# The first transfers, transposes and splits of an input projection by single k-tiles, and the next x transposes inside its first two half-groups

## The chip, the core and the metric

The kernel runs on one core of one Trainium2 chip. Four compute engines work beside each other: TensorE (PE in the rows; its weight loads are PEld), VectorE (DVE), ScalarE (ACT) and GpSimd (POOL). SyncE (SP) issues nearly all DMAs, which 16 DMA engines carry out. The metric is the device time of one execution in microseconds (us), less is better. Times are medians of three runs.

## What is computed

One decoder layer over 256 tokens of width 2048, in float32. The part that matters here is the beginning, the normed input projection:

```python
def rmsnorm(x, g):
    xf = x.astype(jnp.float32)
    r = lax.rsqrt(jnp.mean(xf * xf, axis=-1, keepdims=True) + EPS)
    return (xf * r).astype(x.dtype) * g
...
    h = rmsnorm(x, norm_mix_g[l])
    proj = jnp.einsum('bsd,de->bse', h, w_in[l])
    dq, dk, dv, mq, mk, mv, gate = jnp.split(proj, SPLITS, axis=-1)
```

`w_in` is 2048 x 8192. Behind it follow eight differential-attention heads, eight heads of ordinary causal attention (with 256 tokens there is one block), the gate, an output projection with `w_out`, a cross-attention to `mem` with four heads, and a last RMSNorm. All of that is the same before and after.

## The kernel before, in words

**Three products for one.** A float32 product is made from rounded parts. Of each weight tile, ScalarE makes `w_hi` (a rounded copy of `w_raw`) and VectorE makes `w_lo = w_raw - w_hi`. The input x is transposed by TensorE into PSUM; ScalarE scales it by the gain and writes `aT_hi`, and VectorE writes `aT_lo`, the rest. TensorE then adds hi times hi, hi times lo and lo times hi.

**Half-groups.** The contraction over 2048 rows goes by 16 k-tiles of 128. Two k-tiles with 512 columns of weights (512 KB) are a half-group. One pair of heads takes 16 half-groups, numbered n = 0 to 15 in `pair_window`; n = 0 to 7 make q and k, transposed, in `project_qk`: for each of the two k-tiles four matmuls of 512 columns with `w_hi` (L501) and four of 256 columns with `w_lo` (L509). n = 8 to 15 make v and the gate (`half_group`).

**Buffers.** `w_raw` has eight slots of a half-group, `w_hi` and `w_lo` four. SP issues the loads in order in `load_pair_half`, two DMAs of 256 KB for each half-group, one for each block of 256 columns. x comes in five parts, `X_PARTS`, between the loads of weights: 256, 256, 512, 512 and 512 columns.

**Blocks.** x is transposed in four blocks of four k-tiles (`transpose_block`, L483). A block has two banks of PSUM, two k-tiles in each, so eight transposes. `block_made` counts banks that TensorE has transposed, `block_hi` those that ScalarE has done (`block_hi_bank`, L753, two operations of 256 columns), `block_lo` those that VectorE has done (`block_lo_bank`, L971, two operations). A half-group n of the first pair waits in `pair_window` for `block_lo` n + 1: it reads just the two k-tiles of one bank.

**The order at the start.** Every engine runs its own list in order. On TensorE it is: `keep_busy(5)`, which are matmuls on an identity tile that compute nothing (L462), the transpose of the gain, the first bank of x, `keep_busy(4)`, the second bank, `keep_busy(2)`, half-group 0, block 1, half-groups 1 and 2, block 2, half-groups 3 and 4, block 3, and so on. On ScalarE and VectorE a bank of x and the split of a half-group of weights take turns. Only half-group 0 is split by k-tile (L740, L741, L954, L957); its two DMAs count on one semaphore, so both k-tiles wait for both. Behind half-group 7 TensorE transposes the row scales (L589), which VectorE makes from the sums of squares of x. A matmul record of `keep_busy` is half of one call: five calls are ten records.

Of the kernel before, what the change touches and what calls it, by code (L numbers as in the profile page):

```python
# [22 lines left out]
F32 = mybir.dt.float32  # L23
# [69 lines left out]
X_PARTS = ((0, 256), (256, 512), (512, 1024), (1024, 1536), (1536, 2048))  # L93
WARM_UP = (5, 4, 2)
# [14 lines left out]
def program(nc, x, mem, norm_mix_g, w_in, lambda_q1, lambda_k1, lambda_q2, lambda_k2,  # L109
            subln_g, w_out, norm_mem_g, mem_norm_g, w_q_mem, w_kv_mem, w_o_mem, final_g, out):  # L110
    with ExitStack() as ctx:
# [135 lines left out]
        first_hi = sem("first_hi")  # L247
        first_lo = sem("first_lo")
# [95 lines left out]
        def _(sp):  # L344
# [92 lines left out]
        def _(pe):  # L437
            def half_group(half, slot, banks, hi, lo, k0, first, last):


                first_half = isinstance(half, int) and half == 0
                if first_half:
                    pe.wait_ge(first_lo, 1)
                else:
                    wait(pe, lo_made, half + 1)
                for k in range(GK // 2):
                    if first_half and k == 1:
                        pe.wait_ge(lo_made, 1)
# [15 lines left out]
            def transpose_block(b):  # L464
# [4 lines left out]
                if source == "x" and n > 0:  # L469
                    pe.wait_ge(x_loaded[n + 1], 16)  # L470
# [6 lines left out]
                for i in range(2):  # L477
                    if source == "x" and n == 0:
                        pe.wait_ge(x_loaded[i], 16)
# [6 lines left out]
                    if source == "x" and n == 0:  # L486
                        keep_busy(WARM_UP[1 + i])

            def project_qk(half, slot, k0, first, last):


                first_half = isinstance(half, int) and half == 0
                if first_half:
                    pe.wait_ge(first_hi, 1)
                else:
                    wait(pe, lo_made, half + 1)
                for k in range(GK // 2):
                    if first_half and k == 1:
                        pe.wait_ge(hi_made, 1)
# [3 lines left out]
                    if first_half:  # L503
                        if k == 0:
                            pe.wait_ge(first_lo, 1)
                        else:
                            pe.wait_ge(lo_made, 1)
# [53 lines left out]
            def pair_window(j, kind, first=False):  # L561

                for n in range(PAIR_HALVES):
# [7 lines left out]
                    if n < PAIR_HALVES // 2:  # L571
                        if first:
# [6 lines left out]
                    if first:  # L579
                        if n in (0, 2, 4):  # L580
# [18 lines left out]
            transpose_block(0)  # L599
# [127 lines left out]
        def _(act):  # L727
            def split_hi(half, i, turn, tail=False):

                act.wait_ge(half_loaded[i % RAW], 32 * (turn + i // RAW + 1))  # L730
                raw = w_raw[:, i % RAW]
# [6 lines left out]
                if isinstance(half, int) and half == 0:  # L738
# [573 lines left out]
```

## Time and profile before

| | us |
|---|---|
| median of 3 runs | 599.54 (599.49 to 599.58) |
| the profiled execution | 600.03 |
| its span, first to last instruction | 598.2 |
| TensorE busy | 586.5 (98%) |
| TensorE weight loads | 499.3 (83%) |
| VectorE busy | 423.3 (71%) |
| ScalarE busy | 321.2 (54%) |
| first matmul of the projection starts | 8.38 |
| first matmul of half-group 1 starts | 12.19 |
| first matmul of half-group 2 starts | 15.12 |

The profiled execution took 1.83 us more than its span and 0.49 us more than the median. A share of busy time is a mean over all stages; for a change at the start the timeline of the first microseconds and the places where TensorE sits idle say more.

### The profile page before, as it was taken

How to read it: one execution, taken by the hardware profiler on the slowest of the kernel's cores; microseconds unless marked ns; L12 is line 12 of the kernel's file. 1: busy time of each engine (PE TensorE's matmuls, PEld its weight loads, DVE VectorE, ACT ScalarE, POOL GpSimd, SP SyncE). 2: the span in 40 equal slices, each digit the busy share in tenths (PEclk: the TensorE clock that was granted, in tenths of full speed). 3: DMA queues.
4: the chain of work that ended last, by engine and by line, in shares of the span. 5: the costliest groups of instructions: out<-in, count | busy, mean ns of one | idle time of the engine just before them, and what ended most of it. 6: DMA issues, size and time to landing. Idle time of an engine off the chain costs nothing.

```text
span 598.2 us, 9295 instructions
## 1 busy us (share of the span) xinstructions
PE 586.5 (98%) x3070; PEld 499.3 (83%) x3070; DVE 423.3 (71%) x709; ACT 321.2 (54%) x549; POOL 17.6 (3%) x41
## 2 busy tenths in 40 slices
PE   8999999999999999999999999999999999999994
PEld 7888888888888888888888888888888888888883
DVE  4698789779788787487676765856566656655875
ACT  5765555546536645545455454553457565544723
POOL 2001001001000100100100100000000000000000
PEclk9999999999999999999999999999999999999998
DMA  8976555554554556555554657645555555454303
GB/s 274 327 255 204 183 169 166 193 175 150 196 171 155 181 167 210 175 167 168 192 175 145 206 173 262 223 171 188 177 177 176 169 182 195 165 198 147 106 1 141
DMA packets 91261, 108.51 MB, mean 181 GB/s; under 512 B 6962, under 2 KB 73059, under 8 KB 90723
## 3 DMA queue, kind: packets, MB, share of 16 engines
q1 hardware_dynamic: 91202, 108.18, 54.8%
q8 instruction: 14, 0.23, 0.2%
q14 instruction: 13, 0.10, 0.0%
q10 hardware_dynamic: 32, 0.01, 0.0%
HBM read 106.06 MB, written 2.10 MB: 181 GB/s over the span
## 4 chain that ended last, share of the span: by engine, by line
PE 96%; DVE 1%; ACT 1%; DMA 1%; issue 0%; SPq 0%; ACTq 0%; DVEq 0%
PE ps L501 19%; PE ps L452 18%; PE ps L454 18%; PE ps L453 18%; PE ps L509 10%; PE ps L550 2%; PE ps L483 2%; PE ps L708 1%; PE ps L712 1%; PE ps L707 1%; PE ps L524 1%; PE ps L538 1%; DMA xs<-in_x 1%; PE ps L681 1%; PE ps L557 1%; PE ps L661 1%
## 5 line engine op out<-in xcount | busy, mean ns | idle before, releaser
L961 DVE TENSOR_TENSOR w_lo<-w_raw,w_hi 128x1024 fp32r<-128x1024 f32 x187 | 229.0, 1226 | 108.1 <-ACT w_hi L743 106.9
L743 ACT ACTIVATE w_hi<-w_raw 128x1024 fp32r<-128x1024 f32 x187 | 198.2, 1062 | 169.9 <-PE ps L454 92.0
L501 PE MATMUL ps<-aT,w_hi 128*128 128x512 f32 x512 | 141.1, 397 | 0.0
L452 PE MATMUL ps<-w_hi,aT 128*128 128x512 f32 x320 | 126.6, 395 | 0.0
L453 PE MATMUL ps<-w_lo,aT 128*128 128x512 f32 x320 | 124.8, 390 | 0.0
L454 PE MATMUL ps<-w_hi,aT 128*128 128x512 f32 x320 | 124.7, 390 | 0.0
L501 PEld LDWEIGHTS ps<-aT,w_hi 128*128 128x128 f32 x512 | 87.3, 189 | 11.7
L509 PEld LDWEIGHTS ps<-aT,w_lo 128*128 128x128 f32 x512 | 78.4, 189 | 10.9
L509 PE MATMUL ps<-aT,w_lo 128*128 128x256 f32 x512 | 81.3, 281 | 0.0
L454 PEld LDWEIGHTS ps<-w_hi,aT 128*128 128x128 f32 x320 | 60.1, 188 | 12.7
L452 PEld LDWEIGHTS ps<-w_hi,aT 128*128 128x128 f32 x320 | 60.1, 188 | 12.3
L453 PEld LDWEIGHTS ps<-w_lo,aT 128*128 128x128 f32 x320 | 60.1, 188 | 11.9
L452 PE MATMUL ps<-w_hi,yT_hi 128*128 128x512 f32 x128 | 50.7, 396 | 0.0
L454 PE MATMUL ps<-w_hi,yT_lo 128*128 128x512 f32 x128 | 49.9, 390 | 0.0
L453 PE MATMUL ps<-w_lo,yT_hi 128*128 128x512 f32 x128 | 49.8, 389 | 0.0
L998 DVE RECIPROCAL pool<-pool 128x128 f32<-128x128 f32 x32 | 30.5, 953 | 1.1
L783 ACT ACTIVATE pool<-pool,small 128x256 f32<-128x256 f32 (+1 forms) x48 | 21.3, 445 | 16.1 <-DVE small L1037 16.1
L454 PEld LDWEIGHTS ps<-w_hi,yT_lo 128*128 128x128 f32 x128 | 24.0, 188 | 5.1
L453 PEld LDWEIGHTS ps<-w_lo,yT_hi 128*128 128x128 f32 x128 | 24.1, 188 | 4.7
L452 PEld LDWEIGHTS ps<-w_hi,yT_hi 128*128 128x128 f32 x128 | 24.1, 188 | 4.7
L428 POOL TENSOR_TENSOR alibi<-dist,slopes 128x256 f32<-128x256 f32 x16 | 15.7, 1000 | 320.7 <-DVE small L1037 320.7
L971 DVE SCALAR_TENSOR_TENSOR aT<-ps,gainsT,aT 128x256 fp32r<-128x256 f32 x32 | 14.0, 479 | 13.1 <-ACT aT L753 13.1
(168 smaller groups left out, 551.6 us busy)
## 6 DMA issues: line engine op xcount, KB each, us to landing
w_raw<-in_w_in SPq DMA_DIRECT2D x256, 256.0 KB, 2.8
w_raw<-in_w_out SPq DMA_DIRECT2D x64, 256.0 KB, 3.3
w_raw<-in_w_kv_mem SPq DMA_DIRECT2D x32, 256.0 KB, 2.9
w_raw<-in_w_q_mem SPq DMA_DIRECT2D x16, 256.0 KB, 2.9
w_raw<-in_w_o_mem SPq DMA_DIRECT2D x16, 256.0 KB, 3.3
mems<-in_mem SPq DMA_DIRECT2D x1, 2048.0 KB, 10.2
xs<-in_x SPq DMA_DIRECT2D x3, 512.0 KB, 7.5
w_raw<-in_final_g SPq DMA_DIRECT2D x1, 1024.0 KB, 4.7
```

What stands on the lines that cost most here:

```text
L428: pool_e.tensor_tensor(alibi[:, u], dist[:, :], slope, ALU.mult).then_inc(alibi_ready, 1)
L452: pe.matmul(acc, hi[:, k0 + k, tok], w_hi[:, slot, k], start=first and k == 0, stop=False)
L453: pe.matmul(acc, hi[:, k0 + k, tok], w_lo[:, slot, k], start=False, stop=False)
L454: m = pe.matmul(acc, lo[:, k0 + k, tok], w_hi[:, slot, k], start=False, stop=last and k == GK // 2 - 1)
L483: m = pe.transpose(ps[:, bank + i, (k * NT + t) * P:(k * NT + t + 1) * P], rows_of[:, t, col:col + P], ident[:, :])
L501: pe.matmul(ps[:, c, :], w_hi[:, slot, k, c * P:(c + 1) * P], aT[:, k0 + k].rearrange("p i s -> p (i s)"), start=first and k == 0, stop=False)
L509: m = pe.matmul(ps[:, c, 0:SEQ], w_lo[:, slot, k, c * P:(c + 1) * P], aT_hi[:, k0 + k, :], start=False, stop=last and k == GK // 2 - 1)
L743: act.activation(w_hi[:, i % SPLITS], raw, ACT.Copy).then_inc(hi_made, 1)
L783: m = act.activation(prob_sb[:, u, c, cols], prob_sb[:, u, c, cols], ACT.Exp, bias=neg_max[:, u, t, c:c + 1], accum_out=exp_sum[:, c, u, t ...
L961: dve.tensor_tensor(lo, w_raw[:, i % RAW], hi.bitcast(F32), ALU.subtract).then_inc(lo_made, 1)
L971: m = dve.scalar_tensor_tensor(lo, ps[:, bank + i, (k % 2) * SEQ:(k % 2 + 1) * SEQ], gainsT[:, gain:gain + 1], hi.bitcast(F32), ALU.mult, ...
L998: dve.reciprocal(s, s).then_inc(silu_steps, 1)
```

## The change

It touches the first two half-groups of the first pair and the x transposes that come before half-group 2.

- **Transfers.** The first two parts of x are one k-tile each (128 columns, 128 KB), and there are seven parts instead of five. Half-groups 0 and 1 are loaded by k-tile: the first k-tile of each in one DMA of 256 KB with a semaphore of its own (`k_loaded`), the second in two DMAs of 128 KB.
- **Transposes.** The first bank of block 0 is split in two: `transpose_first(0)` ahead of the projection, `transpose_first(1)` behind the first four matmuls of half-group 0. The second bank of block 0 moves behind the four matmuls with `w_hi` of the second k-tile of half-group 0. The first bank of block 1 moves into half-group 1, the second behind it. Blocks 2 and 3 stay.
- **Splits.** ScalarE and VectorE do k-tile 0 of x, k-tile 0 of the weights, k-tile 1 of x, k-tile 1 of the weights, then bank 1 of block 0 and half-group 1, this too by k-tile.
- **Matmuls on the identity tile.** Three calls ahead of the gain's transpose instead of five, four behind the first transposes, and none behind that.

```diff
-X_PARTS = ((0, 256), (256, 512), (512, 1024), (1024, 1536), (1536, 2048))
-WARM_UP = (5, 4, 2)
+X_PARTS = ((0, 128), (128, 256), (256, 512), (512, 768), (768, 1024), (1024, 1536), (1536, 2048))
+X_PART_OF = {(1, 0): 3, (1, 1): 4, (2, 0): 5, (3, 0): 6}
+WARM_UP = (3, 4)
...
+            def load_pair_rows(n, k):
+
+                if k == 0:
+                    sp.dma_start(w_raw[:, n, 0, :].rearrange("p (s c) -> p s c", c=2 * P),
+                                 in_slabs[n][:, 0, 0:2, 0:2 * P]).then_inc(k_loaded[n], 16)
+                else:
+                    for part, slab in enumerate(SLABS["diff", 0]):
+                        sp.dma_start(w_raw[:, n, 1, part * 2 * P:(part + 1) * 2 * P], in_slabs[n][:, 1, slab, 0:2 * P]
+                                     ).then_inc(half_loaded[n], 16)
+
             load_x(0)
-            for n in range(PAIR_HALVES):
+            for n in range(2):
+                load_pair_rows(n, 0)
+                if n == 0:
+                    load_x(1)
+                load_pair_rows(n, 1)
+                load_x(2 + n)
+            for n in range(2, PAIR_HALVES):
                 load_pair_half(DIFF, 0, 0, n)
-                if n in (0, 1, 3, 5):
-                    load_x((n + 1) // 2 + 1)
+                if n in (2, 3, 5):
+                    load_x({2: 4, 3: 5, 5: 6}[n])
...
+            def transpose_first(k):
+
+
+                pe.wait_ge(x_loaded[k], 16)
+                for t in range(NT):
+                    m = pe.transpose(ps[:, 6 - 2 * k, (k * NT + t) * P:(k * NT + t + 1) * P],
+                                     xs[:, t, k * P:(k + 1) * P], ident[:, :])
+                m.then_inc(k_made if k == 0 else block_made, 1)
...
+                early = half if isinstance(half, int) and half < 2 else None
+                if early is None:
                     wait(pe, lo_made, half + 1)
                 for k in range(GK // 2):
+                    if early is not None and k == 0:
+                        if early == 0:
+                            pe.wait_ge(k_block_lo, 1)
+                        pe.wait_ge(k_hi, early + 1)
+                    if early is not None and k == 1:
+                        pe.wait_ge(block_lo, early + 1)
+                        pe.wait_ge(hi_made, early + 1)
                     for c in range(4):
                         pe.matmul(ps[:, c, :], w_hi[:, slot, k, c * P:(c + 1) * P],
                                   aT[:, k0 + k].rearrange("p i s -> p (i s)"), start=first and k == 0, stop=False)
+                    if early == 0:
                         if k == 0:
+                            transpose_first(1)
                         else:
+                            transpose_block(0, (1,))
+                    if early == 1 and k == 0:
+                        transpose_block(1, (0,))
...
-                        if first:
+                        if first and n > 0:
                             pe.wait_ge(block_lo, n + 1)
...
                     if first:
-                        if n in (0, 2, 4):
+                        if n == 1:
+                            transpose_block(1, (1,))
+                        if n in (2, 4):
                             transpose_block(1 + n // 2)
...
             def split_hi(half, i, turn, tail=False):
 
+                raw = w_raw[:, i % RAW]
+                if isinstance(half, int) and half < 2:
+
+                    act.wait_ge(k_loaded[half], 16)
+                    act.activation(w_hi[:, half, 0], raw[:, 0], ACT.Copy).then_inc(k_hi, 1)
+                    if half == 0:
+                        block_hi_first(1)
+                    act.wait_ge(half_loaded[half], 32)
+                    act.activation(w_hi[:, half, 1], raw[:, 1], ACT.Copy).then_inc(hi_made, 1)
+                    return
```

The first rows of TensorE before, from the transpose of the gain to half-group 1 (L483 are transposes of x, L462 the matmuls on the identity tile, L501 and L509 the projection with `w_hi` and `w_lo`; the branch rows of the small loops are the last three of each loop):

```order
L483 MATMUL ps<-ident,xs 128x128 [waits x_loaded1]
L483 MATMUL ps<-ident,xs 128x128 x3
L461 UNCONDITIONAL_BRANCH
L462 MATMUL ps<-ident 128x128
L461 REGISTER_ALU
L461 COMPARE_AND_BRANCH
L501 MATMUL ps<-aT,w_hi 128x512 [waits first_hi,block_lo]
L501 MATMUL ps<-aT,w_hi 128x512 x3
L509 MATMUL ps<-aT,w_lo 128x256 [waits first_lo]
L509 MATMUL ps<-aT,w_lo 128x256 x3
L501 MATMUL ps<-aT,w_hi 128x512 [waits hi_made]
L501 MATMUL ps<-aT,w_hi 128x512 x3
```

Both banks of block 0 are transposed ahead of the first L501, and nothing stands between the groups of half-group 0.

The same place on TensorE now, from the first matmul of half-group 0 to the first of half-group 1 (L484 and L507 are transposes of x, L526 and L541 what L501 and L509 were):

```order
L526 MATMUL ps<-aT,w_hi 128x512 [waits k_hi,k_block_lo]
L526 MATMUL ps<-aT,w_hi 128x512 x3
L484 MATMUL ps<-ident,xs 128x128 [waits x_loaded1]
L484 MATMUL ps<-ident,xs 128x128
L541 MATMUL ps<-aT,w_lo 128x256 [waits k_lo]
L541 MATMUL ps<-aT,w_lo 128x256 x3
L526 MATMUL ps<-aT,w_hi 128x512 [waits hi_made,block_lo]
L526 MATMUL ps<-aT,w_hi 128x512 x3
L507 MATMUL ps<-ident,xs 128x128 [waits x_loaded2]
L507 MATMUL ps<-ident,xs 128x128 x3
L541 MATMUL ps<-aT,w_lo 128x256 [waits lo_made]
L541 MATMUL ps<-aT,w_lo 128x256 x3
```

The two transposes of k-tile 1 stand between k-tile 0's groups, and the four of bank 1 behind the L526 of k-tile 1.

What comes next on TensorE now, half-group 1 up to the first matmul of half-group 2:

```order
L526 MATMUL ps<-aT,w_hi 128x512 [waits k_hi,block_lo]
L526 MATMUL ps<-aT,w_hi 128x512 x3
L507 MATMUL ps<-ident,xs 128x128 [waits x_loaded3]
L507 MATMUL ps<-ident,xs 128x128 x3
L541 MATMUL ps<-aT,w_lo 128x256 [waits k_lo]
L541 MATMUL ps<-aT,w_lo 128x256 x3
L526 MATMUL ps<-aT,w_hi 128x512 [waits hi_made,block_lo]
L526 MATMUL ps<-aT,w_hi 128x512 x3
L541 MATMUL ps<-aT,w_lo 128x256 [waits lo_made]
L541 MATMUL ps<-aT,w_lo 128x256 x3
L507 MATMUL ps<-ident,xs 128x128 [waits x_loaded4]
L507 MATMUL ps<-ident,xs 128x128 x3
```

Block 1, which stood ahead of half-group 1, now stands half inside it and half behind it; half-group 2 follows.

ScalarE before, from its first operation on x to the weights of half-group 2 (L753 is x, the others are weights):

```order
L753 ACTIVATE aT<-ps,gainsT 128x256 [waits block_made,gainsT_ready]
L753 ACTIVATE aT<-ps,gainsT 128x256
L740 ACTIVATE w_hi<-w_raw 128x512 [waits half_loaded0]
L741 ACTIVATE w_hi<-w_raw 128x512
L753 ACTIVATE aT<-ps,gainsT 128x256 [waits block_made]
L753 ACTIVATE aT<-ps,gainsT 128x256
L743 ACTIVATE w_hi<-w_raw 128x1024 [waits half_loaded1]
L753 ACTIVATE aT<-ps,gainsT 128x256 [waits block_made]
L753 ACTIVATE aT<-ps,gainsT 128x256
L743 ACTIVATE w_hi<-w_raw 128x1024 [waits half_loaded2]
```

And ScalarE now (L790 and L801 are x, L769, L773 and L782 weights):

```order
L790 ACTIVATE aT<-ps,gainsT 128x256 [waits k_made,gainsT_ready]
L769 ACTIVATE w_hi<-w_raw 128x512 [waits k_loaded0]
L790 ACTIVATE aT<-ps,gainsT 128x256 [waits block_made]
L773 ACTIVATE w_hi<-w_raw 128x512 [waits half_loaded0]
L801 ACTIVATE aT<-ps,gainsT 128x256 [waits block_made]
L801 ACTIVATE aT<-ps,gainsT 128x256
L769 ACTIVATE w_hi<-w_raw 128x512 [waits k_loaded1]
L773 ACTIVATE w_hi<-w_raw 128x512 [waits half_loaded1]
L801 ACTIVATE aT<-ps,gainsT 128x256 [waits block_made]
L801 ACTIVATE aT<-ps,gainsT 128x256
L782 ACTIVATE w_hi<-w_raw 128x1024 [waits half_loaded2]
```

The weights of half-group 1 still stand behind bank 1 of block 0, and those of half-group 2 behind the first bank of block 1. VectorE has the same order, each operation behind ScalarE's of the same name.

## Rows read from the trace of the kernel before

**Rows 1.** Waits of TensorE over the whole span: us in total, times, longest.

```profile
PE ps L483 <- DMA xs<-in_x: 0.8, 1, 0.8
PE ps L589 <- DVE pool L1138: 0.5, 1, 0.5
```

**Rows 2.** Stretches, us from the start: length, then busy us of each engine.

```profile
8.37:15.10 6.73, 6.73 (x43) 5.86 (x42) 4.76 (x8) 4.94 (x9) 0.00 (x0) 1.00 1.04 349
...
34.75:598.20 563.45, 554.78 (x2886) 471.32 (x2886) 403.07 (x668) 297.87 (x515) 14.49 (x14) 1.00 0.53 174
```

**Rows 3.** Chain that ended last, first microseconds: start, us, what.

```profile
2.28 5.19 DMA xs<-in_x
...
8.62 0.93 PE ps L501 x4
9.55 0.47 PE ps L509 x4
...
11.42 0.87 PE ps L483 x8
```

**Rows 4.** Timeline to 9 us: start, us, engine, line, operation, count [idle before].

```profile
0.75 0.45 SPq L360 DMA_DIRECT2D xs<-in_x  x1
1.25 0.98 SPq L354 DMA_DIRECT2D w_raw<-in_w_in  x2
...
1.74 2.50 PE L462 MATMUL ps<-ident 128*128 128x128 f32 x10 [1.74 <-POOL ident L411]
...
4.38 1.11 PE L483 MATMUL ps<-ident,xs 128*128 128x128 f32 x4
...
5.60 0.84 ACT L753 ACTIVATE aT<-ps,gainsT 128x256 fp32r<-128x256 f32 x2 [2.87 <-PE ps L483]
6.56 0.88 DVE L971 SCALAR_TENSOR_TENSOR aT<-ps,gainsT,aT 128x256 fp32r<-128x256 f32 x2 [1.90 <-ACT aT L753]
6.85 0.63 ACT L740 ACTIVATE w_hi<-w_raw 128x512 fp32r<-128x512 f32 x1 [0.41 <-DMA w_raw<-in_w_in]
...
7.51 0.66 PE L483 MATMUL ps<-ident,xs 128*128 128x128 f32 x4 [0.79 <-DMA xs<-in_x]
...
8.38 1.17 PE L501 MATMUL ps<-aT,w_hi 128*128 128x512 f32 x4
```

**Rows 5.** One DMA each, from issue to landing: size, us (last number).

```profile
xs<-in_x SPq DMA_DIRECT2D x1, 256.0 KB, 2.8
mix_gain<-in_norm_mix_g ACTq DMA_DIRECT2D x1, 8.0 KB, 2.2
...
w_raw<-in_w_in SPq DMA_DIRECT2D x1, 256.0 KB, 3.5
...
w_raw<-in_w_in SPq DMA_DIRECT2D x1, 256.0 KB, 5.1
```

**Rows 6.** Single records of L462, and the core's mean granted clock.

```profile
5.29 0.42 PE L462 MATMUL ps<-ident 128*128 128x128 f32 x1
...
8.01 0.28 PE L462 MATMUL ps<-ident 128*128 128x128 f32 x1
...
core 0: 598.2 us, clock 0.996
```

**Rows 7.** Timeline, 11 to 15.2 us: from block 1 to half-group 2.

```profile
11.26 1.04 PE L483 MATMUL ps<-ident,xs 128*128 128x128 f32 x8
...
11.90 0.84 ACT L753 ACTIVATE aT<-ps,gainsT 128x256 fp32r<-128x256 f32 x2 [1.12 <-PE ps L483]
...
12.65 1.06 ACT L743 ACTIVATE w_hi<-w_raw 128x1024 fp32r<-128x1024 f32 x1
12.77 0.88 DVE L971 SCALAR_TENSOR_TENSOR aT<-ps,gainsT,aT 128x256 fp32r<-128x256 f32 x2 [0.73 <-ACT aT L753]
...
13.75 1.23 DVE L961 TENSOR_TENSOR w_lo<-w_raw,w_hi 128x1024 fp32r<-128x1024 f32 x1
...
15.12 1.17 PE L501 MATMUL ps<-aT,w_hi 128*128 128x512 f32 x4
```

**Rows 8.** Timeline further on: half-group 4's load, and block 3.

```profile
17.00 1.06 ACT L743 ACTIVATE w_hi<-w_raw 128x1024 fp32r<-128x1024 f32 x1 [1.60 <-DMA w_raw<-in_w_in]
...
21.68 1.09 PE L501 MATMUL ps<-aT,w_hi 128*128 128x512 f32 x4
...
25.18 0.84 ACT L753 ACTIVATE aT<-ps,gainsT 128x256 fp32r<-128x256 f32 x2 [0.92 <-PE ps L483]
```

More of the change, by code:

```diff
@@ L246, in program @@
         half_loaded = [sem(f"half_loaded{s}") for s in range(RAW)]
[L247 to L248 removed]
+        k_loaded = [sem("k_loaded0"), sem("k_loaded1")]
+        k_made = sem("k_made")
+        k_block_hi = sem("k_block_hi")
+        k_block_lo = sem("k_block_lo")
+        k_hi = sem("k_hi")
+        k_lo = sem("k_lo")
         hi_made = sem("hi_made")
@@ L438, in half_group @@
             def half_group(half, slot, banks, hi, lo, k0, first, last):
[L441 to L445, printed above, removed]
+                wait(pe, lo_made, half + 1)
                 for k in range(GK // 2):
-                    if first_half and k == 1:
-                        pe.wait_ge(lo_made, 1)
                     for t in range(NT):
@@ L476, in transpose_block @@
                     pe.wait_ge(block_lo, 2 * (before[-1] + 1))
-                for i in range(2):
+                for i in banks:
+                    if (n, i) in X_PART_OF and source == "x":
+                        pe.wait_ge(x_loaded[X_PART_OF[n, i]], 16)
                     if source == "x" and n == 0:
-                        pe.wait_ge(x_loaded[i], 16)
+                        pe.wait_ge(x_loaded[2], 16)
                     for k in range(2):
@@ L737, in split_hi, with block_hi_first @@
                 wait(act, half_done, half - behind + 1)
-                if isinstance(half, int) and half == 0:
-                    act.activation(w_hi[:, 0, 0], raw[:, 0], ACT.Copy).then_inc(first_hi, 1)
-                    act.activation(w_hi[:, 0, 1], raw[:, 1], ACT.Copy).then_inc(hi_made, 1)
-                    return
                 act.activation(w_hi[:, i % SPLITS], raw, ACT.Copy).then_inc(hi_made, 1)
+            def block_hi_first(k):
+                if k == 0:
+                    act.wait_ge(k_made, 1)
+                else:
+                    act.wait_ge(block_made, 1)
+                act.activation(aT_hi[:, k], ps[:, 6 - 2 * k, k * SEQ:(k + 1) * SEQ], ACT.Identity,
+                               scale=gainsT[:, k:k + 1]).then_inc(k_block_hi if k == 0 else block_hi, 1)
             def block_hi_bank(b, i):
@@ L950, in split_lo @@
                 lo = wo_lo[:, i - WO_HALF0] if over_yT else w_lo[:, i % SPLITS]
-                if isinstance(half, int) and half == 0:
-                    dve.wait_ge(first_hi, 1)
-                    dve.tensor_tensor(lo[:, 0], w_raw[:, 0, 0], hi[:, 0].bitcast(F32), ALU.subtract
-                                      ).then_inc(first_lo, 1)
-                    dve.wait_ge(hi_made, 1)
-                    dve.tensor_tensor(lo[:, 1], w_raw[:, 0, 1], hi[:, 1].bitcast(F32), ALU.subtract
+                if isinstance(half, int) and half < 2:
+                    dve.wait_ge(k_hi, half + 1)
+                    dve.tensor_tensor(lo[:, 0], w_raw[:, half, 0], hi[:, 0].bitcast(F32), ALU.subtract
+                                      ).then_inc(k_lo, 1)
+                    if half == 0:
+                        block_lo_first(1)
+                    dve.wait_ge(hi_made, half + 1)
+                    dve.tensor_tensor(lo[:, 1], w_raw[:, half, 1], hi[:, 1].bitcast(F32), ALU.subtract
                                       ).then_inc(lo_made, 1)
```

36 lines of the change are left out of this document (18 added, 18 removed).

## The prediction, made before the changed kernel had run

> **What bounds the kernel now.** I read the waits of TensorE first. After its start it waits only twice: 0.8 us for the second part of x and 0.5 us for the row scales behind half-group 7 [rows 1]. The stretches agree: from 8.37 to 15.10 it is busy all 6.73 us, and of the 563.45 us behind 34.75 us it is idle for 8.67 [rows 2], all of it at the end of the kernel, when no matmul is left. So TensorE sets the time, and a microsecond that its work of the first stage ends sooner or later is a microsecond of the whole.
>
> What the start waits for is in the chain that ended last: the second part of x, issued at 2.28, lands 5.19 us later, at 7.47 [rows 3]. The timeline shows the rest: four transposes at 7.51, two calls on the identity tile, then the first projection matmul at 8.38. The first k-tile's `w_hi` was ready at 6.85 + 0.63 = 7.48 and bank 0 of x at 6.56 + 0.88 = 7.44 [rows 4]. Three things thus came in at the same moment, and the change has to speed up all of them.
>
> The second thing to see is that the engines behind TensorE are nearly as late as it is. Block 1's transposes start at 11.26, ScalarE takes its first bank at 11.90, the weights of half-group 2 at 12.65, VectorE their rest at 13.75, done at 14.98, and half-group 2 starts at 15.12 [rows 7]. TensorE had in that time 0.87 for eight transposes and 2 x (0.93 + 0.47) = 2.80 for half-group 1 [rows 3], 3.67 of 3.86 us. So **from the start of the first bank of block 1 to half-group 2 it takes 3.86 us, whatever TensorE does meanwhile**, because half-group 2's weights stand behind that bank on both engines. The change keeps this order. Half-group 2 is therefore the place to measure at: behind it nothing is moved.
>
> **The change part by part.**
>
> **The start.** Three calls instead of five: ten records took 2.50 us [rows 4], some 0.24 each, six take 1.5 and end at 3.2. The gain's transfer, issued at 0.74, lands 2.2 later at 2.9 [rows 5]; its transpose costs 0.2. The first part of x, 256 KB, landed 0.75 + 2.8 = 3.55 [rows 4, 5]; half of that lands no later, so the two transposes go at 3.5. Four took from 4.38 to ScalarE's 5.60, 1.22 us with records 0.22 apart; two take 0.78, ScalarE starts at 4.3, one operation (0.42) and 0.12 of handing on lead to VectorE at 4.85, its 0.44 to 5.3 [rows 4]. Against that stands the weight's k-tile. Of the two first weight DMAs of 256 KB the one issued at 1.25 landed at 4.75, the one issued 0.5 later at 6.87 [rows 4, 5]. The new k-tile 0 is one DMA at the place of the first. Bounds are thus 4.75 and 6.87, below 4.75 by at most the 0.3 us that 128 KB less in front of it are worth at 349 GB/s [rows 2]; I take 4.75, since its place and its bytes are those of the first. With 0.63 for `w_hi` it is 5.4. The four calls on the identity tile end at 3.95 + 8 x 0.22 = 5.7. First projection matmul: **5.65 instead of 8.38, 2.73 us earlier**.
>
> The Trainium skill ("DMA: Bandwidth & Descriptors", "Rules for kernel authors") speaks against this part: many small transfers should be coalesced. By its fit in "Anatomy of one DMA" (2.0 us fixed, bytes at 436 GB/s) half a part of x would land an estimated 0.3 us sooner and no more; that fit is for another issuing path. By it the sum would be the same, since the transposes at 3.5 stand behind the gain's.
>
> **Clock.** A record on the identity tile takes 0.42 us at 5.29 and 0.28 at 8.01, and the mean granted clock of 0.996 leaves about 0.004 x 598.2 x 2 = 4.8 us at the lower of the two levels, 1.2 GHz [rows 6]: it rose near 5.9, with TensorE at work since 1.74. The new order keeps it at work nearly as long. So 0.3 us of the first four matmuls run at half speed and cost 0.15.
>
> **Half-group 0.** Now each step is followed to the next.
> - Four matmuls from 5.65: 0.93 + 0.15 [rows 3], so k-tile 1's transposes at 6.7. Their x has landed if the third DMA in the queue lands by then: between 4.75 and 7.47 by its neighbours, so 0.8 us is the worst.
> - From these two transposes to the second k-tile's matmuls: a bank of four took 0.64 to ScalarE [rows 7], two 0.42; ScalarE 0.42 + 0.03; VectorE 0.44; 0.14 to TensorE (14.98 to 15.12). Sum 1.45, with k-tile 1's `w_hi`, which stands between on ScalarE (0.5 + 0.6), giving the same within 0.1. I take 1.5: **second k-tile at 8.2**. TensorE has 0.22 + 0.47 for it to do and waits 0.8.
> - Four matmuls, 0.93: bank 1's transposes at 9.13. Their x (cumulated 1 MB, which landed by 7.47 before [rows 3]) is there.
> - Bank 1 to half-group 1: 0.64 + 0.84 + 0.03 + 0.88 + 0.14 = 2.53 [rows 7]. **Half-group 1 starts at 11.66**; TensorE has 0.44 + 0.47 to do, and waits 1.6 us. Before, this bank lay ahead of the first matmul, and its chain was covered by half-group 0.
>
> **Half-group 1.** Four matmuls, so block 1's first bank is transposed at 12.59, against 11.26 before. With the 3.86 us half-group 2 starts at 16.45 against 15.12: **1.33 us later**. TensorE's own work in between is 0.44 + 0.47 + 0.93 + 0.47 + 0.44 = 2.75, so it waits a third time, 1.0 us. In short: 2.73 us are won at the start; 6 more transposes lie behind the first matmul (0.65), and some 3.4 us of waits are new.
>
> **Loads.** SP issues three DMAs more before the weights of half-group 3, about 0.5 us each [rows 4]. The first load that ScalarE had to wait for behind half-group 1 was half-group 4's, at 17.00, while TensorE needed it at 21.68 [rows 8]; with 1.06 + 1.23 for the split there are 2.4 us to spare, and TensorE is later by 1.3 now. The cost is nothing; without that cover it would be 1.5.
>
> **Behind.** The row scales' chain hangs on block 3's transposes: ScalarE stood idle 0.92 for them [rows 8], so it moves as TensorE moves, and the wait of 0.5 stays. The sum against the profiled execution: 600.03 + 1.33 = 601.4, and against the median 599.54 + 1.33 = **600.9**.
>
> **The rivals.**
>
> **Late first transfers, slower still.** If the first k-tile of the weights lands at 6.87, as the second of the old pair did, `w_hi` is ready at 7.5, the first matmul starts at 7.6 (1.95 later than reckoned, less the 0.15), and every step behind moves with it: +3.1, 602.7. It decides from 4.75 on, microsecond for microsecond. For it: packets of all DMAs share the 16 engines, which are full. Against it: its place in the queue. A partial case (landing at 5.5, or k-tile 1's weights at 8) gives +1.9. Chance 0.16.
>
> **The clock rises late.** If the gaps of the new start keep the lower clock through half-group 0, each L501 group costs 0.93 more: twice that in the chain (behind bank 1 only waits follow), less the 0.15, and the handings at 0.2 more, +1.8 to 2 on top at worst; half of it gives +2.4, 601.9. The Trainium skill ("TensorE: Matmul & The Clock Gate", Part 1) says that the throttled state is the default and only activity lifts it, which this trace's rise after continuous work agrees with [rows 6]. Chance 0.06.
>
> **The head start stays, faster.** If bank 1's and k-tile 1's chains were hidden, so that TensorE never waited in half-groups 0 and 1, it would have the first bank of block 1 at 5.65 + 1.62 + 1.84 + 0.93 = 10.04, and half-group 2, by the 3.86, at 13.9: 1.2 earlier, **598.3**. It decides at the start of that bank: before 11.26 the kernel gains, after it it loses. To reach 11.26 the second k-tile has to start at 6.9, 1.3 sooner than the chain of rows gives. For it speaks only that first transfers may land sooner than I think. Chance 0.08.
>
> **About even.** The clock is up from the first matmul and the weights land by 4.4: first matmul at 5.15, second k-tile at 7.58, block 1's first bank at 11.97, +0.7, 600.2; a little more in TensorE's favour gives zero. The middle between this and my sum is as likely as either. Chance of a shift between -0.4 and +0.6: 0.10.
>
> **How the numbers follow.** The forecast's own case (+0.6 to +2.0) has 0.60. About 1.2 us (0.2%) is what a measurement of this kernel can tell from none, and I put 0.40 of the 0.60 above it. Slower: 0.40 + 0.16 + 0.06 = 0.62. Within: 0.20 + 0.08 = 0.28. Faster: 0.08 + 0.02 = 0.10. The range reaches from 599.3, the low end of the even case, to 602.8, the late landing with a little over: it leaves out the head start and more than one mishap together. My likeliest case alone is 600.1 to 601.6.
>
> **What would show it.** First projection matmul near 5.6; a wait of TensorE of about 0.8 us before the second k-tile, put down to VectorE's or ScalarE's work on k-tile 1; one of about 1.6 us before half-group 1, put down to VectorE's L1030; one of 1.0 before half-group 2, put down to L1011; half-group 2 at 16.4. Behind it each start should be later by the same amount, to the end. It is wrong if TensorE shows no wait before half-group 1, or if block 1's first bank is transposed before 11.26, or if the distance from that bank to half-group 2 is not 3.9 us.

## The result, and the profile of the changed kernel

The changed kernel takes 601.46 us (median of 10 runs, 601.12 to 601.96) against 599.90 of the kernel before, measured beside it (10 runs, 599.28 to 600.16). The ratio is 1.0026 with a 95% interval of 1.0018 to 1.0034: it is slower, by 1.1 to 2.0 us. The profiled execution took 601.14 us with a span of 599.3, which is 1.11 us more than the 600.03 of the profiled one before.

The waits of TensorE, which were two before [rows 1] (us in total, times, longest). The first line is the wait at the very start, which both kernels have:

```profile
PE ps L477 <- POOL ident L432: 1.7, 1, 1.7
PE ps L526 <- DVE aT L1030: 1.4, 1, 1.4
PE ps L526 <- DVE w_lo L1011: 0.9, 1, 0.9
PE ps L526 <- DVE aT L1018: 0.7, 1, 0.7
PE ps L623 <- DVE pool L1197: 0.4, 1, 0.4
```

Where the three new ones stand is shown by the timeline of the changed kernel to half-group 2 (start, us, engine, line, operation, count [idle before]), beside [rows 4] and [rows 7]:

```profile
3.54 0.69 PE L484 MATMUL ps<-ident,xs 128*128 128x128 f32 x2
...
4.33 0.47 ACT L790 ACTIVATE aT<-ps,gainsT 128x256 fp32r<-128x256 f32 x1 [1.60 <-PE ps L484]
4.70 0.62 ACT L769 ACTIVATE w_hi<-w_raw 128x512 fp32r<-128x512 f32 x1
4.92 0.48 DVE L1018 SCALAR_TENSOR_TENSOR aT<-ps,gainsT,aT 128x256 fp32r<-128x256 f32 x1 [1.10 <-ACT aT L790]
...
5.46 1.19 PE L526 MATMUL ps<-aT,w_hi 128*128 128x512 f32 x4
...
6.49 0.38 PE L484 MATMUL ps<-ident,xs 128*128 128x128 f32 x2
...
8.04 1.16 PE L526 MATMUL ps<-aT,w_hi 128*128 128x512 f32 x4 [0.70 <-DVE aT L1018]
...
9.04 0.60 PE L507 MATMUL ps<-ident,xs 128*128 128x128 f32 x4
...
11.47 1.20 PE L526 MATMUL ps<-aT,w_hi 128*128 128x512 f32 x4 [1.37 <-DVE aT L1030]
...
12.51 0.60 PE L507 MATMUL ps<-ident,xs 128*128 128x128 f32 x4
...
16.34 1.17 PE L526 MATMUL ps<-aT,w_hi 128*128 128x512 f32 x4 [0.91 <-DVE w_lo L1011]
```

The first projection matmul starts at 5.46 instead of 8.38: 2.92 us are won. Each dependent step then gives some back: half-group 0's second k-tile waits 0.70, half-group 1 waits 1.37 for bank 1 of block 0, half-group 2 waits 0.91 for its weights, and it starts at 16.34 against 15.12 [rows 7], **1.22 us later**. The stretches of the two kernels say the same (length, then busy us of PE, PEld, DVE, ACT, POOL with their instructions, clock, DMA share, GB/s). Between 8.37 and 15.10 TensorE was busy without a gap before [rows 2], and now it is idle for 1.37 of the 6.73 us:

```profile
8.37:15.10 6.73, 5.36 (x35) 4.59 (x34) 3.34 (x8) 3.66 (x7) 0.00 (x0) 1.00 0.97 325
15.10:34.75 19.65, 18.74 (x112) 16.31 (x111) 14.00 (x27) 15.63 (x22) 0.00 (x0) 1.00 1.01 323
```

The row scales are transposed at 35.84 (L623) against 34.75 before, 1.09 later, and the span is 1.1 longer. Behind that nothing differs: in the last 561.9 us of the span TensorE is busy for 553.21 us, and was for 553.23. Here is the place in the timeline of the changed kernel:

```profile
27.09 1.06 ACT L782 ACTIVATE w_hi<-w_raw 128x1024 fp32r<-128x1024 f32 x1
...
28.04 1.91 ACT L891 ACTIVATE pool<-xs 128x2048 f32<-128x2048 f32 x1
...
35.84 0.44 PE L623 MATMUL ps<-ident,pool 128*128 128x128 f32 x2 [0.38 <-DVE pool L1197]
```

### The profile page after: what moved, and what is told of

It reads as the page before. It is cut to its first block, busy times and chain, and to the rows that moved or that the text cites. A ratio compares the mean times of both kernels' runs of the same rounds, so it can differ in the third digit from the quotient of the medians.

```text
span 599.3 us, 9279 instructions
## 1 busy us (share of the span) xinstructions
PE 585.5 (98%) x3062; PEld 497.9 (83%) x3062; DVE 423.5 (71%) x710; ACT 321.1 (54%) x550; POOL 17.6 (3%) x41
## 4 chain that ended last, share of the span: by engine, by line
PE 96%; ACT 1%; DVE 1%; issue 0%; POOL 0%; ACTq 0%; POOLq 0%; DVEq 0%
PE ps L526 19%; PE ps L467 18%; PE ps L469 18%; PE ps L468 18%; PE ps L541 9%; PE ps L582 2%; PE ps L507 2%; PE ps L747 1%; PE ps L743 1%; PE ps L742 1%; PE ps L556 1%; PE ps L570 1%; PE ps L716 1%; PE ps L589 1%; PE ps L696 1%; PE ps L477 1%
## 5 line engine op out<-in xcount | busy, mean ns | idle before, releaser
L782 ACT ACTIVATE w_hi<-w_raw 128x1024 fp32r<-128x1024 f32 x186 | 197.3, 1062 | 167.9 <-PE ps L469 92.0
L526 PE MATMUL ps<-aT,w_hi 128*128 128x512 f32 x512 | 141.3, 397 | 3.0 <-DVE aT L1030 1.4
L526 PEld LDWEIGHTS ps<-aT,w_hi 128*128 128x128 f32 x512 | 87.3, 189 | 15.2 <-DVE aT L1030 1.6
L541 PEld LDWEIGHTS ps<-aT,w_lo 128*128 128x128 f32 x512 | 78.1, 189 | 10.6
L541 PE MATMUL ps<-aT,w_lo 128*128 128x256 f32 x512 | 81.5, 281 | 0.0
```

The costliest lines, as they stand in the source:

```text
L526: pe.matmul(ps[:, c, :], w_hi[:, slot, k, c * P:(c + 1) * P], aT[:, k0 + k].rearrange("p i s -> p (i s)"), start=first and k == 0, stop=False)
L541: m = pe.matmul(ps[:, c, 0:SEQ], w_lo[:, slot, k, c * P:(c + 1) * P], aT_hi[:, k0 + k, :], start=False, stop=last and k == GK // 2 - 1)
L782: act.activation(w_hi[:, i % SPLITS], raw, ACT.Copy).then_inc(hi_made, 1)
```

## The experiments

Ten more runs were made, one of them of the changed kernel again. Two theories stood against each other. The **order theory**, the prediction's: each transpose moved behind a matmul group puts a chain over two other engines in front of the next group, and half-group 2 comes later for that. The **stream theory** came up after the first results: the loads are a chain of their own, which bounds the row scales. In the table, "group 1" is how long the first four projection matmuls took; hg1 and hg2 are the starts of half-groups 1 and 2 and "rows" that of the row scales' transposes, all in us in the profiled execution; "profiled" is its time; the median has its count of runs; the ratio is to the kernel before, run beside them; it comes from all runs and differs from the quotient of the two medians by up to 0.0004. The medians of before beside them were 599.66 for the first four of the ten, 600.02 for the next four, 599.85 for the last two; each of these three sets ran on a chip of its own.

```
kernel                      group 1   hg1    hg2    rows   profiled  median (n)   ratio, 95% interval
before                       1.17    12.19  15.12  34.75   600.03    599.90 (10)
changed                      1.19    11.47  16.34  35.84   601.14    601.46 (10)  1.0026 [1.0018, 1.0034]
after_again                  1.56    11.97  16.84  36.34   601.59    601.97 (5)   1.0038 [1.0024, 1.0052]
bank1_sooner                 1.21    10.54  15.41  35.28   600.54    600.84 (11)  1.0020 [1.0011, 1.0029]
block1_sooner                1.47    11.89  15.15  35.69   601.00    600.57 (11)  1.0016 [1.0007, 1.0025]
both_sooner                  1.28    11.38  14.86  35.85   601.13    600.96 (11)  1.0018 [1.0009, 1.0027]
small_transfers_alone        1.17    12.04  15.47  35.97   601.25    600.90 (12)  1.0011 [1.0001, 1.0020]
both_and_squares             1.75    11.07  14.55  34.41   599.66    599.90 (12)  0.9996 [0.9985, 1.0006]
both_squares_rows_later      1.29    10.32  14.14   **     598.71    598.98 (12)  0.9979 [0.9970, 0.9989]
before_rows_later            1.16    11.58  14.62   **     598.84    599.37 (12)  0.9986 [0.9976, 0.9995]
changed_rows_later           2.05    12.68  17.55   **     601.75    601.75 (7)   1.0028 [1.0017, 1.0040]
fewer_identity_calls         2.07    12.60  17.45  36.97   602.21    602.24 (5)   1.0051 [1.0037, 1.0064]
** behind half-group 8 in these, and not waited for
```

**The same kernel again (after_again).**

> The changed kernel once more, beside its variants on one chip. Both theories: 1.1 to 1.6 us above the kernel before. Half-group 2's first matmul at 16.3, waits of TensorE of 0.7, 1.4 and 0.9 us in half-groups 0 and 1.

Measured: ratio 1.0038, and the same five waits. All that differs in the profile is that the first four matmuls took 1.56 us instead of 1.19 in the other profile, and that everything behind them is later by about as much (hg2 16.84 against 16.34). What that is comes below, under the calls on the identity tile.

**Bank 1 of block 0 sooner (bank1_sooner).** Its transposes stand ahead of the waits of the second k-tile:

```diff
+                    if early == 0 and k == 1:
+                        transpose_block(0, (1,))
...
-                        else:
-                            transpose_block(0, (1,))
```

> The four transposes of bank 1 of block 0 stand ahead of the matmuls of k-tile 1 of half-group 0, not behind them. Order theory (the loss is the chain transposes, ScalarE, VectorE, TensorE that begins where TensorE's list puts each bank): the transposes start at 7.6, when their x lands, half-group 1 at 10.1 instead of 11.5, block 1's first bank at 11.0, half-group 2 at 14.9: 1.4 us less than the changed kernel, within 0.4 us of the kernel before. Rival (smaller transfers and more, shorter operations cost the time themselves): nothing gained, since all of them are still there; 1.1 to 1.6 above before.

Measured: half-group 1 at 10.54, 0.93 sooner than in the changed kernel, its wait 0.5 instead of 1.4. Half-group 2 starts at 15.41, not at 14.9: the four transposes waited 0.68 for their x and went at 8.04, not at 7.6. The order theory holds as far as that. The end doesn't follow: 0.3 behind before at half-group 2, but 1.2 us over it in the median, where at most 0.4 had been expected, and the row scales are waited for 0.7 us instead of 0.4.

**The first bank of block 1 sooner (block1_sooner).** It stands at the end of half-group 0 instead of inside half-group 1:

```diff
-                    if early == 1 and k == 0:
-                        transpose_block(1, (0,))
...
-                        if n == 1:
-                            transpose_block(1, (1,))
+                        if n in (0, 1):
+                            transpose_block(1, (n,))
```

> The first bank of block 1 is transposed ahead of half-group 1's first matmul, inside TensorE's wait, and the second bank stays. Order theory: half-group 1 still starts at 11.5 with its wait of about 0.9, but half-group 2 at 14.5 to 14.9 instead of 16.3, so 1.5 to 1.7 us less than the changed kernel, 0 to 0.5 under the kernel before. Rival (the wait ahead of half-group 1, 1.4 us, is itself the loss, and what stands behind it only follows): at most 0.4 gained.

Measured: the bank is transposed at 10.71 and half-group 2 starts at 15.15 without a wait, level with before. But the median is 0.9 over before: the expectation missed, and TensorE waits 0.9 for the row scales.

**Both together (both_sooner).**

> Both moves together. Order theory: half-group 1 at 10.4, half-group 2 at 14.4, now bounded by the transfers (x of block 1 at 9.95, the weights of half-group 2 at 11.9) and by TensorE's own work; 2.0 us less than the changed kernel, 0.4 to 0.6 us under the kernel before, and the steadiest of the four, since a late rise of TensorE's clock hides in the wait for the transfers. Rival (cost of small transfers and operations): as the changed kernel, 1.1 to 1.6 above before.

Measured: half-group 2 at 14.86, not at 14.4, since TensorE waited 1.4 us for two parts of x. That is **level with before or a little ahead (0.26), and the kernel is still 1.1 to 1.3 us slower**. That can't be the order. The chain that ended last (start, us, what) no longer runs over TensorE in the first 26 us, as it did before [rows 3], but over the loads:

```profile
18.26 8.82 DMA w_raw<-in_w_in
27.13 0.94 issue
28.07 2.00 ACT pool L889 x2
30.93 0.95 ACT w_hi L780
31.91 1.22 DVE w_lo L1009
```

ScalarE waits for half-group 7's weights, in the timeline of both_sooner:

```profile
27.11 1.06 ACT L780 ACTIVATE w_hi<-w_raw 128x1024 fp32r<-128x1024 f32 x1 [0.95 <-DMA w_raw<-in_w_in]
28.07 1.90 ACT L889 ACTIVATE pool<-xs 128x2048 f32<-128x2048 f32 x1
...
35.85 0.44 PE L621 MATMUL ps<-ident,pool 128*128 128x128 f32 x2 [0.92 <-DVE pool L1195]
```

The second sum of squares (L889) stands behind that split on ScalarE, the row scales hang on it, and TensorE waits for them. ScalarE waited for the same load in block1_sooner (0.91) and in bank1_sooner (0.25). Looked at with this in mind, the kernel before has it too. Its timeline, and the second of the two DMAs of half-group 7, which SP issued at 17.33 (size, us to landing):

```profile
w_raw<-in_w_in SPq DMA_DIRECT2D x1, 256.0 KB, 8.7
```

```profile
26.00 1.06 ACT L743 ACTIVATE w_hi<-w_raw 128x1024 fp32r<-128x1024 f32 x1
...
26.97 1.90 ACT L843 ACTIVATE pool<-xs 128x2048 f32<-128x2048 f32 x1
```

17.33 + 8.7 = 26.03 is the start of that split to within the accuracy of the two: the load and ScalarE's earlier work, which ends at 26.02, come in at the same moment. The 0.92 us of [rows 8] are there, but by this reading taking them away alone would have brought nothing in this execution. No kernel tests that by itself.

**The transfers alone (small_transfers_alone).** The kernel before with the transfers of the changed one: its order of work is untouched, and it waits for two parts of x where it waited for one. One thing is not as in the change: the last part of x for block 1 is loaded ahead of half-group 2's weights, not behind them.

```diff
-X_PARTS = ((0, 256), (256, 512), (512, 1024), (1024, 1536), (1536, 2048))
+X_PARTS = ((0, 128), (128, 256), (256, 512), (512, 768), (768, 1024), (1024, 1536), (1536, 2048))
...
-            for n in range(PAIR_HALVES):
+            for n in range(2):
+                load_pair_rows(n, 0)
+                if n == 0:
+                    load_x(1)
+                load_pair_rows(n, 1)
+                load_x(2 + n)
+                if n == 1:
+                    load_x(4)
+            for n in range(2, PAIR_HALVES):
```

> The kernel before, with the change's transfers alone (seven parts of x, half-groups 0 and 1 by k-tile; x of block 1 whole ahead of half-group 2's weights, so that block 1 isn't held up). Transposes, splits and matmuls are those of before. Stream theory (the smaller transfers delay the whole stream of loads, which ends in half-group 7's load; ScalarE's squares of x stand behind that load, and the row scales behind them, and TensorE waits for those): half-group 2 within 0.3 us of 15.1, half-group 7's weights land at 26.5 to 27.0 instead of 26.0, row scales as much later, 0.5 to 1.0 us above before. Rival (the form of the transfers costs nothing, all loss is in the order of transposes): within 0.2 us of before.

Measured: ratio 1.0011 [1.0001, 1.0020], some 0.7 us (0.9 by the medians), barely clear of the scatter. The start gains nothing (first projection matmul 8.36), and the loads come late: half-group 7's second DMA goes out at 17.63 instead of 17.33 and takes 9.6 us instead of 8.7, so ScalarE starts the split 1.23 later than before and the row scales are 1.22 later. (Half-group 2 is 0.35 later too, behind a wait of 0.41 for its weights.) The chain, and ScalarE in the timeline:

```profile
17.63 9.58 DMA w_raw<-in_w_in
27.20 0.02 issue
27.23 0.03 ACT w_hi L765
27.25 0.94 issue
28.19 1.99 ACT pool L865 x2
```

```profile
27.23 1.06 ACT L765 ACTIVATE w_hi<-w_raw 128x1024 fp32r<-128x1024 f32 x1 [0.85 <-DMA w_raw<-in_w_in]
...
35.97 0.44 PE L609 MATMUL ps<-ident,pool 128*128 128x128 f32 x2 [0.89 <-DVE pool L1160]
```

So the small transfers have a price of their own, through the stream. Its size is uncertain, since this landing varies from profile to profile: it was at 26.0 and 25.2 in the two profiles with the transfers of before, and from 25.9 to 27.2 in the ten with the new ones. In the changed kernel the order's loss covers it: its last DMA of half-group 7 lands at 17.91 + 8.8 = 26.71, and ScalarE, late by the order, comes to that split at 27.09 only. The two prices are not added; the larger one shows.

**The squares ahead of the split (both_and_squares).** If the stream bounds the row scales because the squares stand behind half-group 7's split on ScalarE, they have to go ahead of it. To both_sooner:

```diff
-                if n > 0:
+                if n > 0 and n != 5:
                     split_hi(n + 2, n + 2, 0)
...
+                if n == 5:
+                    split_hi(n + 2, n + 2, 0)
```

> The variant with both banks transposed sooner, and on ScalarE the second row block's squares of x ahead of the split of half-group 7, not behind it. Stream theory: half-group 7's load no longer stands ahead of the row scales; ScalarE fills its 0.95 us of waiting with the squares, the row scales' transposes start at 34.9 to 35.0 instead of 35.85: 0.9 us less than the variant with both banks sooner, 0.1 to 0.3 above before. Rival (the row scales are late for another reason, such as VectorE's own chain): nothing gained.

Measured: the row scales at 34.41 instead of 35.85, and the profiled time 599.66 instead of 601.13. The ratio is 0.9996, no different from before: with its head start no longer cut off at that place, the changed start is about even. The expectation was a gain of 0.9; of the 1.44 us at the row scales 0.31 were there at half-group 2 already (14.55 against 14.86), ahead of anything that this edit moves. The squares, in the timeline of both_and_squares:

```profile
25.42 1.91 ACT L889 ACTIVATE pool<-xs 128x2048 f32<-128x2048 f32 x1
...
27.45 1.06 ACT L780 ACTIVATE w_hi<-w_raw 128x1024 fp32r<-128x1024 f32 x1
...
34.41 0.44 PE L621 MATMUL ps<-ident,pool 128*128 128x128 f32 x2 [0.69 <-DVE pool L1197]
```

**And the row scales' transposes later (both_squares_rows_later).** One line more moves them behind half-group 8, where TensorE need not wait for them:

```diff
-                        if n == 7:
+                        if n == 8:
```

> As the variant with both banks sooner and the squares moved, and the transposes of the row scales behind half-group 8 on TensorE, not behind half-group 7. If the row scales were all that kept the won time from the end: half-group 8 starts at about 34.0, no wait between 15 and 40 us, 0.7 to 0.9 us under before. Rival (the scores behind half-group 10 then wait for q and k, or a later load is the next limit): a wait appears behind 36 us and less than 0.4 us is gained.

Measured: 598.98 us, ratio 0.9979 [0.9970, 0.9989]: **faster than both kernels**, by 1.0 us against before (1.3 by the ratio). These are all waits of TensorE that are left:

```profile
PE ps L477 <- POOL ident L432: 1.7, 1, 1.7
PE ps L528 <- DVE w_lo L1011: 0.3, 1, 0.3
PE ps L507 <- DMA xs<-in_x: 0.2, 1, 0.2
```

**The same cure without the change (before_rows_later).** How much of that is the new start's? The kernel before gets the same two edits (squares ahead, row scales behind half-group 8).

> The kernel before, with just the two later moves (squares ahead of half-group 7's split, row scales' transposes behind half-group 8). Its start is untouched. If the wait of 0.5 us for the row scales is hidden: 0.4 to 0.5 us under before. The difference between this one and the variant with all moves is what the new start is worth at the end: 0.3 us if the start's gain now goes through, none or less than none if the loads or the clock take it.

Measured: 599.37 us, ratio 0.9986. So 0.65 of the 1.04 us come without any change of the first transfers. The rest is 0.4 us between two medians whose runs overlap (598.60 to 599.47 against 598.77 to 600.10), and the intervals of the two ratios overlap too: that the single k-tiles bring anything, even in their best order here, is not shown. Which of the two edits brings the 0.65 was not tried either; TensorE's wait for the row scales, 0.5 in [rows 1], is most of it, and moving their transposes alone may have taken that away. In this profile the second part of x landed at 7.00 and not at 7.47 as in [rows 3], and half-group 2 started at 14.62 and not 15.12: the landing of the same DMA differs by 0.5 us between profiles, and starts shouldn't be compared more finely than that.

**The changed kernel with the cure (changed_rows_later).** Here half-group 7's load can't bound the row scales any more, and what is left of the loss is the order's and the start's.

```diff
-                        if n == 7:
+                        if n == 8:
...
-                if n > 0:
+                if n > 0 and n != 5:
                     split_hi(n + 2, n + 2, 0)
...
+                if n == 5:
+                    split_hi(n + 2, n + 2, 0)
```

> The changed kernel with the two later moves alone (squares ahead of half-group 7's split, row scales' transposes behind half-group 8). Its order of transposes is untouched. Order theory: half-group 2 still at 16.3 to 16.8, so only the wait of 0.4 us for the row scales goes: 0.3 to 0.5 us under the changed kernel, and, with the loads out of the way for both, 1.2 to 2 us above the kernel before with the same two moves (0.65 us under before). Rival (the order of transposes matters little, and the loads made the loss): as fast as that kernel within 0.4 us.

Measured: ratio 1.0028, against 0.9986 of before_rows_later: 0.42%, some 2.5 us, between two kernels that differ by the change alone (each measured against the kernel before on its own chip). In the profiles half-group 2 starts at 17.55 against 14.62, 2.93 later, and not all of that is the order: 0.50 is the earlier landing of x in before_rows_later's profile, and 1.21 is what this profile's half-group 2 is behind that of the changed kernel (16.34), with the same three waits as there and a first group of 2.05 us instead of 1.19. The 1.22 that are left are the distance of the first pair of profiles (16.34 against 15.12), which the order's three waits explain. The rival, within 0.4 us, is out. What the cure was to save against the changed kernel can't be seen for that longer first group.

```profile
5.58 2.05 PE L526 MATMUL ps<-aT,w_hi 128*128 128x512 f32 x4
...
7.43 0.63 PE L484 MATMUL ps<-ident,xs 128*128 128x128 f32 x2
7.71 0.82 PE L541 MATMUL ps<-aT,w_lo 128*128 128x256 f32 x4
...
12.68 1.21 PE L526 MATMUL ps<-aT,w_hi 128*128 128x512 f32 x4 [1.36 <-DVE aT L1032]
```

**Fewer calls on the identity tile (fewer_identity_calls).** The first group took between 1.19 and 2.05 us in kernels whose start up to there is the same. A single record of L462 took 0.42 us early and 0.28 later [rows 6], and in the chain of the kernel before four of them take 0.45 us at 8.17, 0.11 each, where the changed start's eight take 1.71 in changed_rows_later, 0.21 each. That is the ratio of TensorE's two clock levels, 1.2 and 2.4 GHz, so the suspect is the moment at which its clock rises. (The granted clock doesn't show it: it reads 1.00 in every stretch of the first 10 us, in all profiles.) Taking work from TensorE ahead of the first projection matmul should push that moment back:

```diff
-WARM_UP = (3, 4)
+WARM_UP = (3, 1)
```

> The changed kernel with one call on the identity tile behind the first transposes instead of four, so TensorE is idle from about 4.5 to 5.4. Clock theory (TensorE's clock rises after it has been at work, and the changed start no longer hides a late rise): the first four matmuls still start at 5.4 to 5.6, but run at the lower level longer, 1.9 us instead of 1.0 to 1.4, or groups behind them too; half-group 2 later by 0.4 to 1.5 us, 0.3 to 1.5 above the changed kernel. Rival (the rise comes at its own time, and these calls do not matter): within 0.2 us of the changed kernel.

Measured: ratio 1.0051, the slowest of all. The first group took 2.07, and the `w_lo` group behind it 1.20 instead of 0.72:

```profile
5.46 2.07 PE L526 MATMUL ps<-aT,w_hi 128*128 128x512 f32 x4 [0.81 <-DVE aT L1018]
7.33 0.63 PE L484 MATMUL ps<-ident,xs 128*128 128x128 f32 x2
7.61 1.20 PE L541 MATMUL ps<-aT,w_lo 128*128 128x256 f32 x4
```

That doesn't show that the calls are worth having. The kernel that ran beside this one, changed_rows_later, has all four calls and shows nearly the same start: a first group of 2.05, the two transposes behind it 0.63, the `w_lo` group 0.82, and half-group 2 at 17.55 where this one has it at 17.45. Its median is 0.5 lower, but it has no wait for the row scales, which is 0.38 here. So three calls fewer cost the `w_lo` group some 0.4 us, which the wait behind it covered, and nothing that can be told at half-group 2. What differs from the other changed starts is that the records reach full speed behind 8 us in both of these, where in the changed kernel's first profile they had reached it before 5.5: its eight records on the identity tile took 1.58 us, against 1.91 in changed_rows_later. The rival (the rise comes at its own time) fits better than the expectation.

## Why the prediction was right, and where it was not

The forecast was 600.9 and slower; the median is 601.46, in the range, and slower by 1.1 to 2.0. By its steps:

- **First projection matmul, 5.65.** It came at 5.46. The first k-tile of the weights landed at 1.25 + 2.8 = 4.05, below the bound of 4.75 less 0.3: it came 0.7 sooner, not at most 0.3 (128 KB at 349 GB/s are nearer 0.38, and that isn't enough either; what brought the rest is open). It changed little, since VectorE's work on x ended at 4.92 + 0.48 = 5.40 and that is what the matmul then hung on, as the prediction's 5.3 for that chain had it. fewer_identity_calls bears it out: with TensorE free from 4.65 its first matmul starts at the same 5.46, put down to VectorE's L1018. The late first transfers, a rival, did not happen.
- **The waits.** Predicted 0.8, 1.6, 1.0 (the last is 1.1 by its own terms, 3.86 less 2.75); measured 0.70, 1.37, 0.91, behind the very instructions named. Starts: second k-tile 8.2, measured 8.04; bank 1 9.13, 9.04; half-group 1 11.66, 11.47; block 1's first bank 12.59, 12.51; half-group 2 16.45, 16.34. The distance from that bank to half-group 2 is 3.83 against the 3.86 that the prediction took from [rows 7], although TensorE's work in between is another. This distance, set by two other engines, carried the forecast, and bank1_sooner and block1_sooner show that both links are causes: the one takes 0.93 off half-group 2's start (15.41 against 16.34, first groups of 1.21 and 1.19), the other 1.69 (15.15 against 16.84, first groups of 1.47 and 1.56). The medians follow: 601.97 for the changed kernel beside them, 600.84 and 600.57 for these.
- **"It moves as TensorE moves, and the wait of 0.5 stays".** In the changed kernel it did: 1.22 later at half-group 2, 1.09 at the row scales, 1.11 in the profiled time.
- **"The cost is nothing", under Loads.** This step failed, and the sum held by luck. It looked at half-group 4's load alone, with 2.4 us to spare. Half-group 7's load had none: it landed as ScalarE became free, and the squares and the row scales were behind it. (SP issues four DMAs more ahead of half-group 3's weights, thirteen instead of nine, not three.) Alone, the transfers cost 0.7 us by the ratio, 1.22 at the row scales in the profile. It didn't show because the order's loss was as large and came at the same place.
- **"A microsecond that its work of the first stage ends sooner or later is a microsecond of the whole".** Right for later, wrong for sooner. In both_sooner half-group 2 is no later than before and the kernel is 1.1 slower. So the rival of the head start (598.3) could not come true by the first transposes alone; its point of decision, block 1's first bank before 11.26, was reached in block1_sooner and both_sooner (10.71 and 10.97), and neither gained.
- **Clock, 0.15.** Mis-sized as a constant, and one of its two reasons was a misreading. The 4.8 us at the lower level, worked out of the mean granted clock, do not lie at the start: in the kernel before the granted clock reads 1.00 over the first 10 us and 0.50 at the end, where TensorE has nothing left to do. From the mean nothing follows for the rise; only the lengths of the records speak for it. In length, period, busy us of the engines, clock, DMA share, GB/s:

```profile
0.00:10.00 10.00, 7.47 (x40) 6.87 (x41) 3.22 (x7) 4.60 (x9) 3.12 (x27) 1.00 0.75 226
...
594.00:596.00 2.00, 0.00 (x0) 0.00 (x0) 0.00 (x0) 0.00 (x0) 0.00 (x0) 0.50 1.05 343
```

  Against the 1.16 of the next such group at 8.04 the slow first group cost 0.03 in one profile (1.19), 0.40 in the other (1.56) and 0.89 in changed_rows_later (2.05). The kernel before hides a late start of full speed behind its wait for x; the changed one does not. That this is why the median moved by 1.56 where the profiled execution moved by 1.11 fits both profiles but is only argued, since the other executions have no trace; their mean granted clocks (0.994 to 0.997) don't go with their times.

What stays open: what sets the moment from which TensorE runs at full speed in an execution; how much of the stream's delay is from four DMAs more and how much from their smaller packets; and which of the two edits behind the start is the cure. No kernel separated these.

## What to carry to other kernels

Before counting a start's gain to the end, look for a second chain that runs beside it and meets it later: here a load whose landing coincided with an engine becoming free, so that the profile named the engine and the idle time before it, and by this reading neither alone would have given anything. Moving work behind the first matmul only helps if its whole chain over the other engines (2.4 us from a bank's transposes to its use here) fits under the matmuls between. And see which in-order engine has a reduction standing behind a load it doesn't need, and which in-order engine waits for that reduction: two small edits there brought 0.65 us, and the rebuilt start, on top of them, 0.4 that is not clear of the scatter.

## What the runs showed of the hardware that was not expected

TensorE comes to full speed at another moment in each execution. The first four 512-column matmuls, started at 5.46 to 5.58 in all kernels with the changed start, took 1.19 to 2.07 us; later groups of the same form take 1.08 to 1.21:

```profile
5.46 1.21 PE L528 MATMUL ps<-aT,w_hi 128*128 128x512 f32 x4
...
5.58 1.56 PE L526 MATMUL ps<-aT,w_hi 128*128 128x512 f32 x4
...
5.58 1.75 PE L528 MATMUL ps<-aT,w_hi 128*128 128x512 f32 x4
```

They are of bank1_sooner, after_again and both_and_squares, whose instructions up to that point are the same. The longest two, 2.05 and 2.07, ran beside each other on one chip, where no shorter one was seen; on the other two the range is 1.21 to 1.56 and 1.29 to 1.75. Whether it goes with the chip is open. And a transfer of 256 KB lands 2.7 to 3.2 us after its issue at 1.25, with one small DMA ahead of it, but 8.3 to 9.6 us after it at 16.5 to 18.3, where the DMA engines are busy for 86 to 96% of the time (17.3 to 27 us, in four profiles). With four more small DMAs at the start, 12 us earlier, the landings there were, against the 26.03 of the kernel before, 0.1 sooner to 1.2 later, 0.6 in the middle, where that kernel's own two profiles differ by 0.8.
